# State space chunks: the capped decay difference computed by ScalarE instead of VectorE

## The reference, cut to what matters

```python
cum = jnp.cumsum(dt * a, axis=1)                  # 32 heads = 4 groups x 8
seg = cum[:, :, None] - cum[:, None, :]
decay = jnp.exp(jnp.where(causal, seg, -jnp.inf))
cb = jnp.einsum('btgn,bsgn->btsg', cf, bf)
w = cb[..., None] * decay * dt[:, None]
y = jnp.einsum('btsge,bsgep->btgep', w, xf)
y = y + jnp.einsum('btgn,bgepn->btgep', cf, state) * jnp.exp(cum)[..., None]
to_end = jnp.exp(cum[:, -1:] - cum) * dt
new_state = (state * jnp.exp(cum[:, -1])[..., None, None]
             + jnp.einsum('bsge,bsgn,bsgep->bgepn', to_end, bf, xf))
```

## Time and profile before

| | |
|---|---|
| median of three runs | 3610.83 us |
| the profiled execution | 3621.03 us |
| its span, first to last instruction | 3619.4 us |
| PE, DVE, ACT, POOL busy | 83%, 42%, 22%, 15% of the span |
| mean granted clock of PE | 0.888 of full |
| the nine chunks | from 2528 to about 2990 us of the span |

### The profile page before, as it was taken

How to read it: one execution, slowest core, us unless ns; L and a number is a source line. 1 busy time by engine, 2 the same in 40 slices (tenths; PEclk the granted TensorE clock), 3 DMA queues, 4 the chain that set the end, 5 groups by cost and what they waited for, 6 DMA issues and landing times. The chain is left out here.

```text
span 3619.4 us, 42927 instructions
## 1 busy us (share of the span) xinstructions
PE 2992.3 (83%) x16859; PEld 2370.3 (65%) x16859; DVE 1537.2 (42%) x2730; ACT 782.4 (22%) x1470; POOL 549.1 (15%) x436
## 2 busy tenths in 40 slices
PE   5984366669988789989989978977799995899899
PEld 5984234347777569957789966744555553699577
DVE  4995334434444310033455552035777673100443
ACT  3210133322222112211232221111222121122211
POOL 2220000012212112101222100000221221021011
PEclk8995688989997899987989989977799997999869
DMA  2110300034430221222032221136423311312131
GB/s 78 48 35 16 91 0 1 1 111 157 145 105 0 79 70 45 82 93 93 1 81 94 88 76 68 67 105 212 133 81 87 104 13 51 107 47 81 72 115 48
DMA packets 243061, 269.76 MB, mean 75 GB/s; under 512 B 44198, under 2 KB 198630, under 8 KB 237683
## 3 DMA queue, kind: packets, MB, share of 16 engines
q1 hardware_dynamic: 223090, 179.16, 16.5%
q0 software_dynamic: 16384, 75.77, 5.9%
q10 hardware_dynamic: 3456, 12.98, 0.9%
HBM read 227.03 MB, written 41.28 MB: 74 GB/s over the span
## 5 line engine op out<-in xcount | busy, mean ns | idle before, releaser
L302 PE MATMUL pp<-HH,WS_part 128*128 128x352 f32 x1776 | 573.7, 323 | 0.0
L300 PE MATMUL pp<-HH,WH 128*128 128x352 f32 x1344 | 436.8, 325 | 40.2 <-POOL WS_part L439 40.2
L301 PE MATMUL pp<-HT_part,WH 128*128 128x352 f32 x1344 | 435.0, 324 | 0.0
L302 PEld LDWEIGHTS pp<-HH,WS_part 128*128 128x128 f32 x1776 | 336.4, 189 | 0.0
L300 PEld LDWEIGHTS pp<-HH,WH 128*128 128x128 f32 x1344 | 254.6, 189 | 42.2 <-POOL WS_part L439 42.2
L2513 PE MATMUL OP<-oWO,YT 128*128 128x512 f32 (+1 forms) x576 | 252.5, 597 | 3.3 <-DVE XE L2640 3.3
L301 PEld LDWEIGHTS pp<-HT_part,WH 128*128 128x128 f32 x1344 | 254.9, 190 | 0.0
L439 POOL TENSOR_TENSOR WS_part<-WS,WH 128x1024 fp32r<-128x1024 f32 x56 | 142.7, 2548 | 653.9 <-ACT WH L390 653.9
L2513 PEld LDWEIGHTS OP<-oWO,YT 128*128 128x128 f32 (+1 forms) x576 | 103.8, 182 | 144.0 <-issue 140.5
L1840 DVE TENSOR_REDUCE xmx<-xS 128x4 f32<-128x1024 f32 x16 | 19.5, 1219 | 376.6 <-PE xS L1801 376.6
L770 DVE SCALAR_TENSOR_TENSOR CV<-GXP,cw,CV x240 | 172.5, 757 | 0.0
(11 more groups left out here) (473 smaller groups left out, 5780.8 us busy)
## 6 DMA issues: line engine op xcount, KB each, us to landing
WS<-x_w_qg SPq DMA_DIRECT2D x32, 512.0 KB, 3.9
HT<-cache_mem_k SPq DMA_DIRECT2D x16, 1024.0 KB, 5.1
HT<-cache_mem_v POOLq DMA_DIRECT2D x16, 1024.0 KB, 5.3
CBt<-cum_scratch SPq DMA_DIRECT2D x8, 2048.0 KB, 10.3
xbc_scratch<-oACC ACTq DMA_DIRECT2D x24, 528.0 KB, 2.7
WS<-o_w_in SPq DMA_DIRECT2D x24, 512.0 KB, 3.7
XT<-xbc_scratch SPq DMA_DIRECT2D x8, 1536.0 KB, 7.5
WS<-e_w_in SPq DMA_DIRECT2D x18, 512.0 KB, 4.0
```

Source lines behind the costliest of these rows:

```text
L300: nc.tensor.matmul(out, wh, xh, start=start, stop=False)
L301: nc.tensor.matmul(out, wh, xl, start=False, stop=False)
L302: return nc.tensor.matmul(out, wl, xh, start=False, stop=stop)
```

## The change

The 32 DVE instructions of a chunk are gone, and with them DVE's wait for `r_es` in front of them. In their place ACT runs 32 instructions, one per head on the same 128x128 block (32x32 in the sample chunk): relu(row's value - CB), with the row's value as the bias (a pointer to one value per partition) and -1 as the scale. This is the negative of the capped difference, so the exponential over each group now has the scale -1. All 32 relus stand ahead of the first of the four exponentials; `r_seg` is now raised and waited for on ACT itself. Lines behind the change are numbered 4 higher on ACT and 2 lower from the DVE edit on.

```diff
@@ ssd_chunks, block.scalar, chunk
                     nc.scalar.activation(te[R, :], te[R, :], ACT.Exp).then_inc(r_ex, 1)
                     nc.scalar.activation(dc[:], dc[:], ACT.Exp).then_inc(r_ex, 1)
                     for g in range(4):
+                        for h in range(g * HP, (g + 1) * HP):
+                            ins = nc.scalar.activation(CB[R, h, R], CB[R, h, R], ACT.Relu, bias=cus[R, h:h + 1], scale=-1.0)
+                        ins.then_inc(r_seg, 1)
+                    for g in range(4):
                         act.wait_ge(r_seg, n * 4 + g + 1)
-                        nc.scalar.activation(CB[R, g * HP:(g + 1) * HP, R], CB[R, g * HP:(g + 1) * HP, R], ACT.Exp)\
+                        nc.scalar.activation(CB[R, g * HP:(g + 1) * HP, R], CB[R, g * HP:(g + 1) * HP, R], ACT.Exp, scale=-1.0)\
                             .then_inc(r_ex, 1)
@@ ssd_chunks, block.vector, chunk
                     N.tensor_tensor(te[R, :].unsqueeze(2), CB[R, :, T - 1:T], cus[R, :].unsqueeze(2), ALU.subtract)\
                         .then_inc(r_es, 1)
-                    dve.wait_ge(r_es, n * 2 + 2)
-                    for g in range(4):
-                        for e in range(HP):
-                            h = g * HP + e
-                            ins = N.tensor_scalar(CB[R, h, R], CB[R, h, R], cus[R, h:h + 1], 0.0, ALU.subtract, ALU.min)
-                        ins.then_inc(r_seg, 1)
                     dve.wait_ge(r_tb, n + 1)
```

## The result

The changed kernel takes 3635.06 us (median of 20 runs, 3626.75 to 3647.01), the kernel before 3611.39 us in the same sessions (20 runs, 3603.47 to 3630.47). The ratio is 1.0064, 95% interval 1.0051 to 1.0077: slower by about 23 us. The forecast was slower by 8.4, range up to 3630; the direction is right, the size is a third of what came, and the time lies outside the range.

A forecast was written before the change was run, and what follows sets the result against it. The prediction took the round of DVE's path to the additions and PE's work behind them as the bound; 0.7 (chunk 0) + 4.3 (wait) + 3.4 (clock) = 8.4 us on the median 3610.83 gave 3619.2, range 3609 to 3630.

The forecast's parts named there:

- The loop through DVE's path and PE's second pair of groups: A round is DVE's path from the transposes to the additions, then PE's from the second pair to the transposes.
- The relu's price: On ACT: one relu starts 0.26 us after another, so 32 take 8.32 and DVE's products start 0.72 us later.
- The rival of 0.14: Relus on ACT start every 0.28 us, +1.36 per chunk, chunk 1 late too: +18.5, 3629 us; chance 0.14.
- Chunk 0: PE stands 9.8 us for the first product, so this chunk takes the path's 0.72 us in full.
- Chunk 1: First product 2.81 us later, where DVE had waited 2.88 for PE: costs nothing, 0.07 to spare.
- The rival's fall of the clock: The 0.14 chance rival put chunk 1 late by 0.6 us and into the low clock for the first time (+0.6 + 3.4).
- Chunks 2 to 7, the wait: PE's wait in front of the second pair of groups grows by 0.72 us per chunk: 6 x 0.72 = 4.3.
- Chunks 2 to 7, the clock: Three of six chunks get the 10 us half-clock stretch instead of one: 2 x 1.7 = 3.4 us, between 0 and 8.5.
- The sum: Over the chunks: 0.7 + 4.3 + 3.4 = 8.4 us slower, 3619.2 against the median.
- Sample chunk: Products start about 2.1 us later, but the additions had waited 2.27 us for PE: cost 0.
- Rival 3: Relus every 0.217 us or less: PE's wait and low clock vanish in chunks 2 to 7, about -27, 3584; chance 0.07.

The follow-up runs named there:

- the best split of the capping: Kernel before with groups 0 and 1 capped on DVE, groups 2 and 3 by relu on ACT: 3580.10 us against 3613.10, ratio 0.9918.
- the kernel with both orders changed: Changed kernel with each group's exponential right behind its 8 relus and DVE's XE ahead of the four products: 3586.73 us against 3613.10, ratio 0.9927.

## Why the prediction was wrong, point by point

- **What bounds the chunks: right.** The loop through DVE's path and PE's second pair of groups, and the price of the wait by the clock, are what the experiments show.
- **The relu's price: the step that failed.** The prediction took 0.26 us from one start to the next; it is 0.292. The row it rested on had an ACTIVATION_READ_ACCUMULATOR behind the activation with the pointer, not another such activation. That ACTIVATION_READ_ACCUMULATOR started 0.11 us before the activation's end; the next relu starts about 0.095 before the end of the one ahead of it (387 ns of duration in the trace, 0.292 apart). The like instruction also lasted 0.37, not 0.387. Each chunk's path grew by 1.71 us instead of 0.72. The rival of 0.14, with a relu every 0.28 us, was the nearer one; it was priced at 3629 from rows, and the measured 3635 lies beyond it. By the figures of the Trainium skill, page "ScalarE: Activation LUTs", section "What ACT_TABLE_LOAD costs", a relu starts every 0.294 us, an estimate, and the trace agrees to 2 ns. The prediction set this aside, and priced it at 3632.
- **Chunk 0:** the path's 1.7 is there (PE's first wait is 11.4 us, 9.8 before); the chunk lost 2.3. The other 0.7 (2.33 less 1.66) is not in that wait; where it comes from stays open.
- **Chunk 1:** forecast free, with 0.07 us to spare. At 0.292 the spare is gone: a wait of 0.71. The rival's fall of the clock behind that wait did not come. The chunk lost 1.6; about 0.7 of it lies ahead of the wait, where the transposes between chunks 0 and 1 take longer on PE (3.87 and 2.51 us, before 3.50 and 1.91), a place that the prediction put at nothing.
- **Chunks 2 to 7, the wait:** 6 x 0.72 = 4.3 forecast, 6 x 1.82 = 10.9 measured (2.46 - 0.64). Mis-sized by the relu alone.
- **Chunks 2 to 7, the clock:** 3.4 forecast, with three of six stretches long; all six were, and chunks 2 to 7 lost 17.7 - 10.9 = 6.8 by it. That is within the range of 0 to 8.5 that was given. The run with the path lengthened on DVE has waits of 2.40 to 2.43 us and a long stretch in all six chunks too, so a wait of this length goes with the long stretch there too, without the relus.
- **The sum:** of the 13.3 us between 8.4 forecast and 21.7 found in the chunks, the path and wait of chunks 0 and 2 to 7 are 7.6, the clock 3.4, chunk 1 is 1.6 and the rest of chunk 0 is 0.7.
- **Sample chunk:** free, as forecast: PE's group products still stand right behind its output product there.
- **Rival 3** was the right reading of the other side: the run without the pointer brought relus of 0.200 and 36 us less than the kernel before (31 by the ratio, 20 to 43 by its interval). The prediction put it at 27 less, which is inside that interval; by the traces the chunks are 26.4 us shorter (396.4 against 422.8), so its price of a vanished wait was right.

## What to carry to other kernels

Work moved from a busy engine to an idle one gains nothing when it stays on the same chain and that chain gets no shorter: compare the length of the chain on both engines, not the loads, and a start-to-start distance only from pairs of the same instruction. Before moving work, ask what the waiting engine could do in its wait: one matmul moved into 0.65 us of PE's wait brought 24 us where the change lost 23, and no less, within the intervals, than the best split of the capping. Where a wait drags a stretch at half clock behind it, price the wait with that stretch: here 0.65 us cost 4 us per chunk.

## What the runs showed of the hardware that was not expected

POOL and DVE held each other up here. POOL's product of XK took 10.14 us before and takes 3.62 in the changed kernel, where DVE stands idle at that time; with XE moved ahead, the two start together and DVE's XE takes 5.71 us instead of 2.28. POOL before (chunk 2), and then POOL and DVE of the kernel with both orders changed (chunk 2):

```profile
2649.66 10.14 POOL L2494 TENSOR_TENSOR XK<-XK,Db 128x2048 f32<-128x2048 f32 x1 [13.28 <-DVE XD L2666]
```

```profile
2631.15 3.62 POOL L2494 TENSOR_TENSOR XK<-XK,Db 128x2048 f32<-128x2048 f32 x1 [7.00 <-DVE XD L2663]
...
2631.20 5.71 DVE L2668 TENSOR_TENSOR XE<-XD,te 128x2048 f32<-128x2048 f32 x1
```

In the second, XE, begun 0.05 us after POOL, ends 2.1 us after POOL does, about its own 2.28. In the first, DVE's products had begun 0.16 us ahead of POOL (2649.50), and POOL ends at 2659.80, 3.56 us after DVE's last instruction with both inputs in SBUF (XE, followed at 2656.24), about its own 3.62. So in these two cases the one that began first held the other up until its run was done. The Trainium skill, page "SBUF — State Buffer", section "Who interferes with whom", says that a DVE instruction with two SBUF inputs contends with a GpSimd instruction that reads SBUF, and calls the pair of ports they share an exclusive lock. The trace agrees: 5.71 us against 2.28, and 10.14 against 3.62. With XE moved no time was lost by it, since DVE had 8 us to spare at that place.

A wait of 0.26 us or 0.71 us left the clock at 2.4 GHz (XE moved; chunk 1 of the changed kernel, and of the one with the exponentials interleaved), while 0.65 us in chunks 2 to 7 of the kernel before brought it down each time. So the length of the wait alone does not decide it; what else does, these runs leave open.
